# First mixer of a two-block transformer kernel: decay rows ahead of and between the gate tiles, and two chunks of modulation weights requested ahead of the Fourier constants and used behind the gate

## What is computed

```
mod = silu(c) @ w_ada + b_ada            # shifts, scales and gates, 6 x 1024, for latent and context
h = modulate(rmsnorm(x)); u, z, q, k, v, beta, g = split(h @ w_in)     # q, k, v also: conv, silu, l2norm
for each direction (forward, backward), chunk of tokens, head:
    decay[i, j] = exp(gc[i] - gc[j]) for i >= j, else 0      # gc: running sum of g
    A = strict(beta * K K^T * decay);  T = (I + A)^-1
    v_new = T (beta * V) - T (beta * K * exp(gc)) S;  o = Q exp(gc) S + (Q K^T * decay) v_new
    S = S exp(g_last) + (K exp(g_last - gc))^T v_new
y = concat(real(fft2(u)) @ w_fourier, rmsnorm(o) * silu(z)) @ w_out
x = x + gate * rmsnorm(y)                # then a convolutional feed-forward, then the second block
```

## Time and profile before

| what | value |
|---|---|
| median of three runs | 1630.27 us |
| the profiled execution's own time | 1630.96 us |
| span in its profile | 1629.2 us |
| PE busy | 1336.2 us (82% of the span) |
| VectorE, ScalarE, GpSimd busy | 592.7, 431.3, 213.2 us |
| mean granted TensorE clock | 0.895 of full |
| DMA | 528.44 MB, mean 324 GB/s |

### The profile page before, as it was taken

The page is one execution under the profiler, slowest core; times in us unless marked ns, Lnnn a source line. Parts: engine busy times, 40 slices in busy tenths (PEclk is TensorE's granted clock), DMA queues, the critical chain, the costliest instruction groups (busy, mean ns, idle before and its releaser), DMA issues.

```text
span 1629.2 us, 21694 instructions
## 1 busy us (share of the span) xinstructions
PE 1336.2 (82%) x9444; PEld 875.1 (54%) x9444; DVE 592.7 (36%) x1148; ACT 431.3 (26%) x643; POOL 213.2 (13%) x119
## 2 busy tenths in 40 slices
PE   6999899999999997676666668999977666776678
PEld 3887698999999943122122214999712221221226
DVE  4777655886167411011011004686201101100116
ACT  3554255444453310000000002584200000000005
POOL 0216224786410100000000000000000000000000
PEclk9999899999999898788788789999988878877789
DMA  9306453444647999999999999459899999999992
GB/s 402 146 1 269 189 216 139 173 174 143 217 168 285 378 388 426 427 427 426 428 427 427 426 427 409 173 207 352 347 428 428 426 428 426 426 428 426 428 409 103
DMA packets 52625, 528.44 MB, mean 324 GB/s; under 512 B 4784, under 2 KB 4912, under 8 KB 20144
## 3 DMA queue, kind: packets, MB, share of 16 engines
q1 hardware_dynamic: 51952, 525.22, 78.5%
q10 hardware_dynamic: 576, 1.79, 0.3%
HBM read 525.94 MB, written 1.05 MB: 323 GB/s over the span
## 4 chain that ended last, share of the span: by engine, by line
PE 54%; DMA 37%; DVE 4%; SPq 3%; ACT 2%; issue 1%; POOL 0%; DVEq 0%
PE bank L669 26%; PE bank L1272 9%; DMA ring<-in_w_up 8%; DMA work<-in_w_gate 7%; DMA ring<-in_w_down 7%; DMA ring<-in_w_gate 5%; DMA work<-in_w_down 4%; DMA work<-in_w_up 4%; PE bank L1292 4%; PE bank L1354 3%; SPq L563 3%; PE bank L889 2%; PE bank L1422 2%; DMA ring<-in_dense 2%; PE bank L662 2%; PE bank L741 1%
## 5 line engine op out<-in xcount | busy, mean ns | idle before, releaser
L1272 PE MATMUL bank<-ring,work 128*32 128x512 f32 x1232 | 320.3, 733 | 135.7 <-DMA ring<-in_w_up 70.8
L669 PE MATMUL bank<-work_rounded,ring_rounded 128*128 128x256 f32 (+1 forms) x2000 | 304.8, 287 | 2.2 <-DVE work_rounded L2072 1.2
L669 PEld LDWEIGHTS bank<-work_rounded,ring_rounded 128*128 128x128 f32 x2000 | 267.0, 189 | 9.6 <-issue 2.9
L669 PE MATMUL bank<-xn_rounded,ring_rounded 128*128 128x256 f32 (+1 forms) x1472 | 249.2, 285 | 1.2 <-DVE xn_rounded L2106 1.2
L1272 PEld LDWEIGHTS bank<-ring,work 128*32 128x32 f32 x1232 | 69.7, 130 | 307.6 <-issue 114.5
L2682 DVE TENSOR_TENSOR work<-work,bank 128x512 f32<-128x512 f32 x16 | 11.0, 687 | 542.5 <-PE bank L1272 542.5
L669 PEld LDWEIGHTS bank<-xn_rounded,ring_rounded 128*128 128x128 f32 x1472 | 203.4, 188 | 5.4 <-issue 2.7
L1272 PE MATMUL bank<-work 128*32 128x512 f32 x496 | 155.2, 673 | 32.4 <-DMA work<-in_w_gate 17.6
L1961 POOL TENSOR_TENSOR ring_rounded<-ring,ring_rounded 128x2048 fp32r<-128x2048 f32 (+1 forms) x35 | 148.9, 4271 | 161.5 <-ACT ring_rounded L1495 161.5
L1495 ACT ACTIVATE ring_rounded<-ring 128x2048 fp32r<-128x2048 f32 (+1 forms) x76 | 133.0, 1795 | 51.8 <-PE bank L669 30.3
L1292 PE MATMUL bank<-ring,work 128*32 128x512 f32 x576 | 126.8, 671 | 17.1 <-DMA ring<-in_w_down 17.1
(11 more groups left out here) (340 smaller groups left out, 1752.0 us busy)
## 6 DMA issues: line engine op xcount, KB each, us to landing
ring<-in_dense SPq DMA_DIRECT2D x47, 2048.0 KB, 8.6
ring<-in_w_up SPq DMA_DIRECT2D x38, 2048.0 KB, 30.2
ring<-in_w_gate SPq DMA_DIRECT2D x36, 2048.0 KB, 29.4
ring<-in_w_down SPq DMA_DIRECT2D x34, 2048.0 KB, 29.1
work<-in_w_gate SPq DMA_DIRECT2D x16, 2048.0 KB, 23.0
work<-in_w_down SPq DMA_DIRECT2D x16, 2048.0 KB, 32.4
spare<-in_w_gate SPq DMA_DIRECT2D x8, 2048.0 KB, 29.1
work<-in_w_up SPq DMA_DIRECT2D x8, 2048.0 KB, 32.7
```

What stands on the lines that cost most here:

```text
L669: last = mm(out, rv(high_store[r][:, at:at + P]), rv(x[part][k]), start=opens and k == 0 and j == 0, stop=closes and k == n_k - 1 and j == 2)
L1272: ins = mm(out[slots(y), :], xg[:, k, slots(y)], expert_columns(w, at, 512), start=k == 0, stop=k == KT - 1)
```

## The change

- `decay_rows(3)` and `beta_rows(2)` go ahead of z; z's first half is computed as two single tiles (`latent_tile`), one behind `beta_rows(2)` and one behind `decay_rows(4)` and `(5)`; z's second half goes behind `beta_rows(6)`. The row banks become (6, 0, 7, 1, 6, 3, 7, 0).
- Behind z PE runs the first two `ada1` chunks, the transposes of v, the query products, u, the other two `ada1` chunks, `dft_w`, the transposes of k and `dft_b`; it goes on as before. The uses `vtok` come ahead of `u`.
- SyncE requests `ada1` chunks 0 and 1 ahead of the Fourier constants. `ada1` goes to rings 1, 2, 1, 2 and `ada2` to 0, 1, 2, 0; `kd` moves to ring 1. The hold until `ds_mm` 6 passes from the second chunk of w_out (ring 0) to the first of w_up (ring 1).
- VectorE takes difference 3 ahead of key matrix 1, and the two halves of the u weights' low part stand apart, behind key matrix 2 and behind key matrix 3; its transposes also wait for all of z; it clears `solved` itself; `begc` goes behind the solve.
- ScalarE clears the other two tiles (`tmat_zero`), copies z's second half after its loop, and then v's transposes ahead of u. GpSimd clears nothing and scales the values block by block.

```diff
@@ -96,7 +96,7 @@
...
 
-USES = [("ada0", 4), ("kv", 4), ("q", 2), ("v", 4), ("z", 2), ("u", 2), ("dft_w", 2), ("vtok", 4), ("ktok", 4), ("dft_b", 4),
+USES = [("ada0", 4), ("kv", 4), ("q", 2), ("v", 4), ("z", 2), ("vtok", 4), ("u", 2), ("dft_w", 2), ("ktok", 4), ("dft_b", 4),
         ("dft_y", 2),
@@ -154,7 +154,7 @@
...
             free[first[f"ada{part}"] + c] = ("ada_mm", 4 * (part - 1) + c + 1)
-    for c, last in enumerate((4, 6, 10, 12, 14)):
+    for c, last in enumerate((4, 6, 10, 12, 18)):
         free[first["w_in"] + c] = ("dense_full", use["kv"] + last)
@@ -179,7 +179,7 @@
...
 
-    held_until = {(first["w_out"], 3): ("vn_mm", 1), (first["w_out"] + 1, 0): ("ds_mm", 6),
+    held_until = {(first["w_out"], 3): ("vn_mm", 1), (first["w_up"], 1): ("ds_mm", 6),
                   (first["w_up"] + 1, 2): ("o_mm", 4),
@@ -195,7 +195,7 @@
...
             elif name in ("ada1", "ada2"):
-                r = (c + (1 if name == "ada1" else 2)) % (LOAD_SLOTS - 1)
+                r = ((1, 2, 1, 2) if name == "ada1" else (0, 1, 2, 0))[c]
             elif name == "w_out_b":
@@ -251,7 +251,7 @@
...
     "gate_cols", "gc_exp", "kk_mm", "g_rows", "b_rows", "g_diff", "g_masked", "decay", "qd_exp", "att_exp",
-    "at_ready", "qk_mm", "att_ready", "solved", "tt_zero", "diag_act", "diag_pool", "scaled_v", "qd_ready",
+    "at_ready", "qk_mm", "att_ready", "solved", "tmat_zero", "diag_act", "diag_pool", "scaled_v", "qd_ready",
     "kd_ready", "ks_mm", "rest_ready",
@@ -339,7 +339,7 @@
...
     vnew = ring[2][:, 2048:3072].rearrange("p (d h t) -> p d h t", d=2, h=HEADS)
-    kd = ring[0][:, 0:3072].rearrange("p (e h t) -> p e h t", e=6, h=HEADS)
+    kd = ring[1][:, 0:3072].rearrange("p (e h t) -> p e h t", e=6, h=HEADS)
     attnT, qd = (x.rearrange("p (k s t) -> p k s t", k=KT, s=2)[:, :, 0].rearrange("p (e a) (b t) -> p e a b t", e=4, b=2)
@@ -543,7 +543,10 @@
...
                                  up[0:TOGETHER][:, :, 0:CHUNK // 4].rearrange("e p c -> p e c")).then_inc(S["spare_full"], 16)
-                for c in range(name == "w_in" or name.startswith("ple"), count):
+                if name == "fourier":
+                    for c in range(2):
+                        load(FIRST["ada1"] + c, t["dense"][seen + count + c], CHUNK)
+                for c in range(2 if name == "ada1" else name == "w_in" or name.startswith("ple"), count):
                     load(base + c, t["dense"][seen + c][:, 0:size], size)
@@ -860,6 +863,17 @@
...
 
+        def latent_tile(stage, c, b, i):
+
+            use, chunk, n = USE[stage] + b, FIRST["w_in"] + c, SEQ
+            if i == 0:
+                released(pe, use - BANKS)
+            for k in range(KT):
+                split_arrived(chunk, k)
+                last = split_product(bank[use % BANKS][:, n * i:n * i + n], chunk, 2 * b + i, x_lat, k)
+            if i:
+                assert signal(last, "dense_full") == use + 1
+
         for b in range(2):
@@ -909,7 +923,7 @@
...
 
-        row_bank = (6, 0, 7, 1, 6, 2, 7, 3)
+        row_bank = (6, 0, 7, 1, 6, 3, 7, 0)
         pe.wait_ge(S["gate_cols"], 1)
@@ -924,44 +938,44 @@
...
         beta_rows(0)
-        latent_half("z", 3, 0)
         released(pe, USE["v"] + 3)
...
         beta_rows(2)
+        latent_tile("z", 3, 0, 0)
         pe.wait_ge(S["at_ready"], 1)
         decay_rows(4)
-        latent_half("z", 3, 1)
-        released(pe, USE["z"])
         decay_rows(5)
+        latent_tile("z", 3, 0, 1)
         pe.wait_ge(S["at_ready"], 3)
...
         beta_rows(4)
-        released(pe, USE["z"] + 1)
+        pe.wait_ge(S["g_diff"], 2)
         decay_rows(7)
...
         beta_rows(6)
-        latent_half("u", 4, 0)
-        latent_half("u", 4, 1)
-        arrived(pe, FIRST["fourier"])
+        pe.wait_ge(S["qd_exp"], 2)
+        latent_half("z", 3, 1)
         pe.wait_ge(S["qd_exp"], 4)
-        for x, name in enumerate(("cos_c", "nsin_c")):
-            dense(USE["dft_w"] + x, [(0, 512, [(fo(name), fo("w_f"))])])
-
+        pe.wait_ge(S["at_ready"], 5)
+        ada_rows(1, (0, 1))
+        token_major("vtok", vc)
         pe.wait_ge(S["at_ready"], 8)
...
         query_products(3, 5)
-
-        token_major("vtok", vc)
+        latent_half("u", 4, 0)
+        latent_half("u", 4, 1)
+        ada_rows(1, (2, 3))
+        arrived(pe, FIRST["fourier"])
+        for x, name in enumerate(("cos_c", "nsin_c")):
+            dense(USE["dft_w"] + x, [(0, 512, [(fo(name), fo("w_f"))])])
         token_major("ktok", kc)
-        ada_rows(1, (0, 1))
         for x in range(2):
...
 
-        ada_rows(1, (2, 3))
         ada_rows(2, (0,))
@@ -1616,24 +1630,28 @@
...
             d, u = e % 2, token_of(e // 2, e % 2)
-            if e in (3, 5):
-                to_sbuf("z", e // 4, wk("zs", 512, 512 * (e // 4)))
+            if e == 5:
+                to_sbuf("z", 0, wk("zs", 512))
             if e >= 4:
                 act.wait_ge(S["g_diff"], e + 1)
-                signal(act.activation(qd[:, e - 4], paired(by_head(bank[(6, 2, 7, 3)[e - 4]])), ACT.Exp), "qd_exp")
+                signal(act.activation(qd[:, e - 4], paired(by_head(bank[(6, 3, 7, 0)[e - 4]])), ACT.Exp), "qd_exp")
             act.wait_ge(S["g_masked"], e + 1)
...
 
+        to_sbuf("z", 1, wk("zs", 512, 512))
+        for u in range(4):
+            to_sbuf("vtok", u, wk("vtok", 512, 512 * u))
         for b in range(2):
             to_sbuf("u", b, wk("oT", 512, 512 * b))
+        nothing = c_cols[:, 0, 0:1]
+        signal(act.activation(ring[LOAD_SLOTS][:], nothing.to_broadcast([P, CHUNK]), ACT.Copy), "tmat_zero")
         for x in range(2):
             to_sbuf("dft_w", x, fo_w[:, x])
-        for stage, tile in (("vtok", "vtok"), ("ktok", "ktok")):
-            for u in range(4):
-                to_sbuf(stage, u, wk(tile, 512, 512 * u))
+        for u in range(4):
+            to_sbuf("ktok", u, wk("ktok", 512, 512 * u))
 
@@ -1642,10 +1660,12 @@
...
             to_sbuf("dft_b", x, fo_b[:, x // 2, x % 2].rearrange("p g e -> p (g e)"))
+        act.wait_ge(S["dense_full"], USE["dft_b"] + 4)
+        signal(act.activation(wk("oT"), nothing.to_broadcast([P, 1024]), ACT.Copy), "tmat_zero")
+        ada_rows(1)
         functions(SILU)
...
         functions(LN_EXP)
-        ada_rows(1)
         for b in range(2):
@@ -1654,8 +1674,7 @@
...
             signal(act.activation(p5[high_block, :, 2 * s:2 * s + 2], x, ACT.Copy), "join_act")
-        act.wait_ge(S["tt_zero"], 2)
-        act.wait_ge(S["tt_zero"], 3)
+        act.wait_ge(S["tmat_zero"], 2)
         act.wait_ge(S["solved"], 1)
@@ -1977,24 +1996,19 @@
...
             pool.tensor_tensor(x, x, heads(neg[:, 0]), (ALU.add, ALU.subtract)[d]).then_inc(S["g_masked"], 1)
-        pool.wait_ge(S["dense_full"], USE["z"] + 2)
-        pool.memset(solved, 0.0).then_inc(S["tt_zero"], 1)
         for e in range(4):
...
             pool.tensor_tensor(qd[:, e], qd[:, e], paired(qc[:, :, columns_of(u)]), ALU.mult).then_inc(S["qd_ready"], 1)
-        pool.wait_ge(S["dense_full"], USE["u"] + 2)
-        pool.memset(ring[LOAD_SLOTS][:], 0.0).then_inc(S["tt_zero"], 1)
         for u in range(4):
             released(pool, USE["vtok"] + u)
-        for d in range(2):
-            for u in range(4):
+        for u in range(4):
+            for d in range(2):
                 pool.tensor_tensor(xv[d][:, u], vtok[:, u], bc(beta[:, u, 4 * d:4 * d + 4], shape), ALU.mult)\
                     .then_inc(S["scaled_v"], 1)
-        pool.wait_ge(S["dense_full"], USE["dft_b"] + 4)
-        pool.memset(wk("oT"), 0.0).then_inc(S["tt_zero"], 1)
         pool.wait_ge(S["solved"], 2)
-        pool.wait_ge(S["tt_zero"], 3)
+        pool.wait_ge(S["tmat_zero"], 2)
+        pool.wait_ge(S["scaled_v"], 8)
         for q in range(2, 4):
@@ -2310,7 +2324,7 @@
...
         dve.wait_ge(S["gate_cols"], 2)
-        row_bank, key_bank = (6, 0, 7, 1, 6, 2, 7, 3), (4, 5, 4, 5)
+        row_bank, key_bank = (6, 0, 7, 1, 6, 3, 7, 0), (4, 5, 4, 5)
 
@@ -2334,17 +2348,19 @@
...
         key_matrix(0)
+        difference(3)
         key_matrix(1)
-        weights_low(FIRST["w_in"] + 4)
-        for e in range(3, 8):
-            difference(e)
-            key_matrix(e - 1)
-        key_matrix(7)
-        dve.wait_ge(S["gc_exp"], 1)
-        for d in range(2):
-            last = v.scalar_tensor_tensor(begc[:, d], beta[:, :, 4 * d:4 * d + 4], -1.0, egcol[:, d], ALU.mult, ALU.mult)
-        signal(last, "gate_cols")
-
+        key_matrix(2)
+        weights_low(FIRST["w_in"] + 4, (0,))
+        difference(4)
+        difference(5)
+        key_matrix(3)
+        weights_low(FIRST["w_in"] + 4, (1,))
+        difference(6)
+        key_matrix(4)
+        difference(7)
+        for e in range(5, 8):
+            key_matrix(e)
 
@@ -2355,6 +2371,7 @@
...
         dve.wait_ge(S["at_ready"], 8)
+        dve.wait_ge(S["dense_full"], USE["z"] + 2)
         flat_amat = spare[:].rearrange("p (g t) -> p t g", t=P)
@@ -2367,7 +2384,7 @@
...
```

(9 more changed lines are left out.)

## The result

The changed kernel took 1618.01 us (median of four runs, 1617.83 to 1619.29) against 1630.72 us for the kernel before: ratio 0.9917, 95% interval 0.9905 to 0.9929. It is 12.7 us faster, where 7.8 were forecast. The profiled execution took 1619.29 us (span 1617.5), 11.7 less than the one before. In two later sessions the same pair gave 0.9927 [0.9913, 0.9941] and 0.9928 [0.9911, 0.9945], a gain of 10.8 us each time.

A forecast was written before the change was run, and what follows sets the result against it. PE's progress through the first mixer was taken to set the start of all that follows. 6.6 us at the join (180.58 to 174.0) plus 1.2 of slow clock gave 7.8 off 1630.27: 1622.5 us, range 1618.0 to 1626.5.

The forecast's parts named there:

- the gap: Before the last beta rows: VectorE's u weights' low part and GpSimd's masks take turns, so PE stands 1.9 us.
- Key matrices: VectorE's gate stage: with decay rows early and z in smaller pieces, the eighth ends at about 128.4 us, against 135.5.
- The slower clock behind the gap: PE behind its stand before the last beta rows: the slower clock was kept, 1.5 us; z ends at about 132.1 us.
- the clear: Before the modulation rows: ACT's second clear, 0.95 us, delays them by some 0.5 us, which PE waits.
- Solve and DMA: Before the join: the solve meets two scalings (1.5 us), its transpose ends near 171.2 us; both DMA stands go.
- Rival B: At the join: the solve still bounds and the slow clock behind the stand stays; 5.2 us gained, 1625.1 us; chance 0.13.
- After the join: Behind the join: with no stand before it, the 1.2 us of slow clock there should go too.
- The rigid shift: From the up projection on: later stages last as long as before, so all that follows moves as one block.
- The range: Whole kernel: 1618.0 to 1626.5 us with rivals A and B; the forecast alone spans 1620.5 to 1625.
- Rival A: Gate stage: no gap, PE runs through; join at 170.6 us, 11.2 us gained, 1619.1 us; chance 0.20.

The follow-up runs named there:

- the run with the longer stand: The changed kernel with VectorE's key matrix 4 ahead of its difference 6 instead of behind it; 1621.51 us, ratio 0.9945 to the kernel before.
- the run with the constants first: The changed kernel with modulation chunks 0 and 1 requested behind the Fourier constants again; 1636.41 us, ratio 1.0022 to the kernel before.

## Why the prediction was wrong

Direction, mechanism and bound were right; the gain was undersized, by 3.9 us between the profiled executions and 4.9 between the medians. Two terms of the sum failed, and both are TensorE's clock: 1.5 us kept for a slow stretch behind the gap, where the changed kernel's profiles show none, and nothing for the router, which came out 1.7 us shorter. Some of the miss is a draw: in the two later sessions the gain was 10.8 us, inside the stated range, while the 12.7 of the first lie just beyond its largest gain of 12.3.

*Key matrices and the gap.* Right: done at 128.4 us as forecast; VectorE's weights end at 120.9 (forecast 121.0), POOL's second mask about 122.0 (122.2), the beta rows start at 123.86 us (124.0). That POOL is held as well, which no row of before showed, is now shown: a mask of 1.28 us lasted 3.33 with nothing behind it in the run with the longer stand, and 2.50 for two once the weights' low part was elsewhere. The Trainium skill, SBUF — State Buffer, section Who interferes with whom, says that the order of issue decides which of the two engines is blocked. The traces agree: here the low part ran first and the mask waited, in the solve GpSimd's operations ran and the steps waited.

*The slower clock behind the gap.* This is the step that failed ahead of the join: 1.5 us of it were kept by the sentence "I keep the slower clock behind it too", from one profile. It did not fall there in any profile of the changed kernel, and behind the same 2.00 us in the kernel before it fell in two of five. z was done at 130.6 instead of 132.1 us. Whether the somewhat shorter stand or the execution decides is open. Over all profiles it fell behind none of six stands of 1.6 us, two of six of 2.00, the one of 2.37 and four of six of 2.96 to 2.98 us. The Trainium skill, TensorE: Matmul & The Clock Gate, section What's actually happening, says that the watch on PE's activity is free-running and does not start anew with the kernel. Falls that come in some executions only are what that would give; no run here controls the phase.

*Gap and the clear.* 1.63 us instead of 1.9, as PE came 0.1 later and the rows were ready 0.1 earlier; and 0.27 instead of 0.5 us behind ACT's clear, which took 1.05. From z's end to the join it was 41.4 us with the wait in it; the forecast was 41.9. With z's 1.5 this is all of the 2.0 us at the join.

*Solve and DMA.* Right in what counts: two to three slow steps, clear 0.91 (0.95 taken), the transpose's end at 169.9 instead of 171.2 (z's 1.5 us), no DMA stand. The `begc` products, priced at 1.25 us, took 0.23 us behind the solve; nothing hung on it. Rival B was 1.9 us away, as the scalings put back into the solve show: PE at the join at 171.9, the solve at 173.8 us.

*After the join.* The fall right behind the join is gone (the chunk there takes 1.92 instead of 3.17 us), as forecast. A second one, clock 0.50 at 196 to 200 us in the kernel before, is as deep and now at 184 to 192 us. By the up projection 0.7 us of the 1.2 were left. This stretch took 84.42, 83.50 and 82.69 us in the three profiles of the changed kernel and 85.16 and 84.21 in the two of the kernel before, so a difference of half a microsecond tells nothing.

*The rigid shift.* Right for the projections (290.50 and 290.49 us) and the memory stage; wrong for the router, where 1.7 us fell to the changed kernel by the clock. The sentence "the later stages as long as before" put this at nothing, and it is the second step that failed. That what comes late stays late is shown by the run with the constants first: its first expert product came 16.6 us later (577.4 instead of 560.8 us), and the stretch behind took 1058.8 us, within the spread of all the others. The last 0.7 us are noise of the stretch behind: it took 1055.8 to 1060.5 us in eighteen profiles, with and without the change. The step from 11.7 to 12.7 us is that the profiled execution was the slowest of the four.

*The range.* Rival A had the time, 1619.1 us, without its mechanism: the gap was there. The range's low end lies 1.1 us below it, so it allowed for A's 3.4 us and for next to nothing in the stretches behind the join, though the earlier trace rows showed a clock that moves.

## What to carry to other kernels

Ask first which of two chains is ahead at a join, and by how much: here a filled gap and an earlier request, each alone, were worth nothing while the solve set the join, and moving eight side products out of the solve was worth 1.9 us at the join out of the 5.9 that they cost. Read this lead from more than one profile: it was 1.86 us in one of the kernel before and gone in two others with the same order. A clock loss seen behind a stand in one profile is a term with a chance, not a fixed price; and every stretch of small products behind the change is such a term too, so the range has to hold them. Where PE stands in such a stretch, a product whose result nobody uses may be worth more than its time.
